# Page groups one slot ahead of the scan, first loads over three queues, last scan pair moved into the GLU

## What is computed

```
# S5: diagonal complex recurrence per group and state
x_re, x_im = cf * (B u);  first step += ab * h0
h[t] = ab * h[t-1] + x[t];  y = Re(C h) + d * u
z = gelu(y) @ w_glu + b_glu;  out = z[:, :D] * sigmoid(z[:, D:])
# compression: 8 samples x 2 pairs of KV heads, once for K, once for V
h = b1 + sum over 32 taps of rows(16 n + t) @ w1[t];  out = gelu(h) @ w2  (K: then rope)
```

## Time and profile before

| | |
|---|---|
| median of 3 runs | 3571.66 us (3571.52 to 3574.16) |
| profiled execution | 3578.02 us, its span 3576.2 us |
| TensorE, VectorE, ACT, GpSimd busy | 93%, 56%, 41%, 12% |
| mean granted TensorE clock | 0.968 |

### The profile page before, as it was taken

One profiled execution on the slowest core, in us unless ns is written; L12 is line 12 of the kernel. 1 busy time (PEld: TensorE's weight loads), 2 busy tenths in 40 slices (PEclk: granted clock), 3 DMA queues, 4 the chain that ended last, 5 costly groups with the idle time before them and its releaser, 6 DMA issues.

```text
span 3576.2 us, 71349 instructions
## 1 busy us (share of the span) xinstructions
PE 3333.5 (93%) x27932; PEld 3153.2 (88%) x27932; DVE 2019.8 (56%) x2324; ACT 1482.8 (41%) x1947; POOL 443.1 (12%) x381
## 2 busy tenths in 40 slices
PE   3999999999899999999999997888899999999998
PEld 2888888889899999999989985754689999999997
DVE  5888878765644444445664535344464444444565
ACT  2455555543444433343444431233344443334342
POOL 0555556510000000000000000000000000000000
PEclk9999999999999999999999998988899999999998
DMA  4444544445466556665455556776646655566543
GB/s 113 126 128 141 155 138 147 138 149 171 138 182 184 180 182 178 181 177 180 155 170 173 167 170 199 256 239 215 213 155 180 180 175 185 177 182 180 179 157 109
DMA packets 380155, 608.11 MB, mean 170 GB/s; under 512 B 52875, under 2 KB 138894, under 8 KB 379406
## 3 DMA queue, kind: packets, MB, share of 16 engines
q1 hardware_dynamic: 356878, 549.58, 50.5%
q10 hardware_dynamic: 23056, 55.55, 4.8%
HBM read 594.83 MB, written 26.94 MB: 174 GB/s over the span
## 4 chain that ended last, share of the span: by engine, by line
PE 74%; DVE 11%; issue 5%; POOL 4%; ACT 2%; DMA 2%; SPq 1%; ACTq 0%; POOLq 0%; DVEq 0%
PE psum L372 21%; PE psum L374 21%; PE psum L373 21%; DVE rows_rest L1134 2%; PE psum L2034 1%; DVE turned L1193 1%; PE psum L2085 1%; DMA w_raw<-in_cache_slc_k 1%; PE psum L1932 1%; PE psum L2044 1%; POOL prod_pool L1335 1%; PE psum L856 1%; DVE sumsq L448 1%; PE psum L858 1%; PE psum L857 1%
## 5 line engine op out<-in xcount | busy, mean ns | idle before, releaser
L357 DVE TENSOR_TENSOR w_rest<-w_raw,w_head 128x1024 fp32r<-128x1024 f32 x780 | 980.8, 1270 | 1061.6 <-ACT w_head L353 1056.2
L353 ACT ACTIVATE w_head<-w_raw 128x1024 fp32r<-128x1024 f32 x780 | 816.8, 1057 | 1082.5 <-PE psum L374 1029.2
L372 PE MATMUL psum<-act_head,w_head 128*128 128x264 f32 x4224 | 1209.9, 286 | 29.1 <-DVE act_rest L425 24.8
L374 PE MATMUL psum<-act_head,w_rest 128*128 128x264 f32 x4224 | 1206.6, 286 | 0.0
L373 PE MATMUL psum<-act_rest,w_head 128*128 128x264 f32 x4224 | 1205.0, 285 | 0.0
L372 PEld LDWEIGHTS psum<-act_head,w_head 128*128 128x128 f32 x4224 | 802.1, 190 | 33.3 <-issue 32.3
L373 PEld LDWEIGHTS psum<-act_rest,w_head 128*128 128x128 f32 x4224 | 804.0, 190 | 0.0
L374 PEld LDWEIGHTS psum<-act_head,w_rest 128*128 128x128 f32 x4224 | 802.3, 190 | 0.0
L372 PE MATMUL psum<-hid_head,w_head 128*128 128x264 f32 x1408 | 401.0, 285 | 0.0
L374 PE MATMUL psum<-hid_head,w_rest 128*128 128x264 f32 x1408 | 400.6, 285 | 0.0
L373 PE MATMUL psum<-hid_rest,w_head 128*128 128x264 f32 x1408 | 399.9, 284 | 0.0
(11 more groups left out here) (350 smaller groups left out, 4120.5 us busy)
## 6 DMA issues: line engine op xcount, KB each, us to landing
w_raw<-in_ffn_w_gate SPq DMA_DIRECT2D x176, 512.0 KB, 3.8
w_raw<-in_ffn_w_up SPq DMA_DIRECT2D x176, 512.0 KB, 4.3
w_raw<-in_ffn_w_down SPq DMA_DIRECT2D x176, 512.0 KB, 4.2
w_raw<-in_cache_cmp_k SPq DMA_DIRECT2D x256, 128.0 KB, 2.6
w_raw<-in_cache_cmp_v SPq DMA_DIRECT2D x256, 128.0 KB, 2.7
w_raw<-in_ssm_w_glu SPq DMA_DIRECT2D x64, 512.0 KB, 3.9
w_raw<-in_ple_w_gate SPq DMA_DIRECT2D x64, 512.0 KB, 4.3
w_raw<-in_kv_w SPq DMA_DIRECT2D x48, 512.0 KB, 4.0
```

The lines of the kernel that those rows point to most:

```text
L353: nc.scalar.activation(WH[:, u.slot, :], RAW[:, u.slot, :], ACT.Copy).then_inc(head_done, 1)
L357: nc.vector.tensor_tensor(WL[:, u.slot, :], RAW[:, u.slot, :], WH[:, u.slot, :].bitcast(F32), ALU.subtract).then_inc(rest_done, 1)
L372: nc.tensor.matmul(o, WH[:, u.slot, w], heads[:, k, :], start=k == 0, stop=False)
L374: last = nc.tensor.matmul(o, WL[:, u.slot, w], heads[:, k, :], start=False, stop=k == UK * kunits - 1)
```

## The change

- **Lead of one.** `LEAD` goes from 0 to 1: slot k now holds scan pair k-1. The loop starts at slot 0, with tap group 0 in it; page group 0 is turned in the start. Pair 31 is left over: its inputs are multiplied in slot 31, and its scan, rotation and outputs run behind the splits of the GLU's units (`glu_dve`), with `outputs_pe` at chunk 11.
- **Loads.** SP keeps identity, A, log dt, page table, iota and the state, then the pages. ACT issues x in four column quarters, the samples and the taps (into a buffer of their own, so that the page ring is free). GpSimd issues sixteen: gains, biases, masks, the second weights and rope tables.
- **The start's work.** x is copied out half by VectorE, half by ACT; squares are summed by 16 matmuls with ones in place of four VectorE reductions; tap rests go to GpSimd; the parameter chain is cut in four pieces that lie between the page rests, its last piece (`coefficients_dve`) in slot 0.
- **Order in a slot.** B and C are turned after part 2 instead of after part 1, and ACT copies them after the sines and heads 4 and 5.
- **The end.** The splits of y are spread through slot 31 and the embeddings are turned in two pairs. The final states are turned in the GLU's second step.

```diff
     def start_pe(pe):
...
+        def x_job(c):
+            if c % 4 == 0:
+                pe.wait_ge(ld_x[c // 4], 32 if c == 0 else 16)
+            if c >= 3:
+                if c - 3 < X_BY_DVE:
+                    pe.wait_ge(x_evac_dve, c - 2)
+                else:
+                    pe.wait_ge(x_evac_act, c - 2 - X_BY_DVE)
+            sl = slice(c * P, (c + 1) * P)
+            turn(x_bank(c), [(XN[:, 0, sl], 0), (XN[:, 1, sl], P), (XS[:, sl], 2 * P)]).then_inc(x_turned, 1)
+        def sums(g):
+            pe.wait_ge(sq_first, g + 1)
+            for c in range(4 * g, 4 * g + 4):
+                last = nc.tensor.matmul(PSUM[:, SUM_BANK, 0:T], ONES[:, :], SQ[:, c, :], start=c == 0, stop=c == KC - 1)
...
+        turn(7, [(AN[:, k, :], k * NQ) for k in range(3)]).then_inc(tp_done, 1)
+        for c in range(X_BY_DVE):
+            x_job(c)
+        pe.wait_ge(ld["s0"], 32)
...
+        for c in range(X_BY_DVE, KC):
+            x_job(c)
+        pe.wait_ge(ones_done, 1)
+        for g in range(4):
+            sums(g)
+            turn_pages_pe(pe, 0, 2 * g, 2 * g + 2)
+        pe.wait_ge(ld["vec"], L_VEC)
+        pe.wait_ge(x_evac_act, KC - X_BY_DVE)
+        turn(4, [(VEC[:, 0, :], 0)])
+        turn(5, [(VEC[0:50, 1, :], 0)]).then_inc(tp_done, 1)
+        pe.wait_ge(tp_evac, 3)
+        pe.wait_ge(rows_padded, 2)
     def start_dve(dve):
...
+        turns_step_dve(dve)
...
+        rests_dve(dve, 0, 0, 4)
+        turns_low_dve(dve)
+        rests_dve(dve, 0, 4, 6)
+        turns_high_dve(dve)
+        rests_dve(dve, 0, 6, 8)
+        dve.wait_ge(tp_done, 4)
...
+        rms_dve(dve, "mix0")
     def start_act(act):
+        for q in range(4):
+            sl = slice(q * 512, (q + 1) * 512)
+            act.dma_start(XN[:, :, sl], io["x_prompt"][0].rearrange("(q p) d -> p q d", p=P)[:, :, sl]).then_inc(ld_x[q], 16)
...
+        for g in range(4):
+            nc.scalar.activation(SQ[:, 4 * g:4 * g + 4, :], X[:, 4 * g:4 * g + 4, :], ACT.Square).then_inc(sq_first, 1)
+        for u in range(RING):
+            act.wait_ge(raw_ready[u], 16)
+            nc.scalar.activation(WH[:, u, :], TAPS_FIRST[:, u, :], ACT.Copy).then_inc(head_done, 1)
+            heads_act(act, 0, 2 * u, 2 * u + 2)
+        rms_act(act, "mix0")
+    def start_pool(pool):
...
+        for u in range(RING):
+            pool.wait_ge(head_done, u + 1)
+            nc.gpsimd.tensor_tensor(WL[:, u, :], TAPS_FIRST[:, u, :], WH[:, u, :].bitcast(F32), ALU.subtract).then_inc(rest_done, 1)
...
-    LEAD = 0
+    LEAD = 1
     def stage1_pe(pe):
-        rms_pe(pe, "mix0")
-        pe.wait_ge(ld["late"], L_LATE)
-        for k in range(-1, NITEM):
+        for k in range(NITEM):
             p = k - LEAD
             taps_pe(pe, k, 0)
             turn_pages_pe(pe, k + 1, 0, 2)
             taps_pe(pe, k, 1)
             turn_pages_pe(pe, k + 1, 2, 4)
-            if p >= 1 and p % 2 == 1:
-                turn_bc_pe(pe, p // 2 + 1)
+            if k == NITEM - 1:
+                turn_embeds_pe(pe, 0, DEPTH)
             taps_pe(pe, k, 2)
             turn_pages_pe(pe, k + 1, 4, 6)
             if k == NITEM - 1:
-                turn_embeds_pe(pe)
+                turn_embeds_pe(pe, DEPTH, 2 * DEPTH)
+                second_pe(pe, k - 1)
+            if p >= 1 and p % 2 == 1:
+                turn_bc_pe(pe, p // 2 + 1)
             taps_pe(pe, k, 3)
...
     def stage1_act(act):
...
             heads_act(act, k + 1, 2, 4)
-            if p >= 1 and p % 2 == 1:
-                take_bc_act(act, p // 2 + 1)
...
             heads_act(act, k + 1, 4, 6)
             if boundary:
                 split_taps_act(act, 1)
+            if p >= 1 and p % 2 == 1:
+                take_bc_act(act, p // 2 + 1)
...
     def stage1_dve(dve):
...
             rests_dve(dve, k + 1, 0, 2)
+            if k == 0:
+                coefficients_dve(dve)
             round_dve(dve, p + 1)
+            if final:
+                for c in range(6):
+                    y_rest_dve(dve, c)
+                first_units_dve(dve, 0)
             scans_dve(dve, p)
             rests_dve(dve, k + 1, 2, 4)
             if boundary:
                 split_taps_dve(dve, 0)
+            rotated_out_dve(dve, p)
             if final:
-                first_units_dve(dve, 0)
-            rotated_out_dve(dve, p)
+                rests_embeds_dve(dve, 0, DEPTH)
+                for c in range(6, 12):
+                    y_rest_dve(dve, c)
+                first_units_dve(dve, 1)
...
     def stage1_pool(pool):
         pool.wait_ge(arg_ready, N_PAR)
+        pool.wait_ge(norm_sum, 1)
+        pool.wait_ge(ld["late"], L_LATE)
...
     def glu_pe(pe):
         def first(k):
-            if k == 4:
+            if k == 0:
+                pe.wait_ge(cmp_rest, 8 * NITEM + 2 * DEPTH)
+                pe.wait_ge(cmp_out, NITEM - 1)
+                pe.wait_ge(cmp_gelu, NITEM - 1)
+            if k == 3:
                 second_pe(pe, NITEM - 1)
+            if k == 11:
+                outputs_pe(pe, NPAIR - 1)
+            if k == 12:
+                pe.wait_ge(cmp_out, NITEM)
+            pe.wait_ge(xl_done, k + 1)
...
     def glu_dve(dve):
         def split(eng, u):
+            c = u.n - ph.base - RING
             split_rest(eng, u)
-            if u.n == ph.base + RING + 4:
+            if c == 0:
+                scans_dve(eng, NPAIR - 1)
+            if c == 1:
+                rotated_out_dve(eng, NPAIR - 1)
+            if c == 2:
+                joined_out_dve(eng, NPAIR - 1)
+            if c == 3:
+                y_sum_dve(eng, KC - 1)
+            if c == 4:
+                y_rest_dve(eng, KC - 1)
+            if c == ph.per + 4:
+                dve.wait_ge(cmp_kept, 16 * NITEM)
                 states_dve(eng, 0, 4)
```

More of the change, by code:

```diff
@@ L595, in job, with x_bank, turn @@
+    SUM_BANK = 3
+    def x_bank(c):
+        return 4 + c % 3
+    def start_pe(pe):
+        def turn(bank, ins):
             for src, at in ins:
                 n, m = src.shape[0], int(np.prod(src.shape[1:]))
-                last = nc.tensor.transpose(PSUM[0:m, j % 8, at:at + n], src, IDENT[0:n, 0:n])
-            last.then_inc(tp_done, 1)
-            j += 1
-        pe.wait_ge(ld["const"], L_CONST)
-        job([(VEC[:, 0, :], 0)], (ld["vec"], L_VEC))
-        job([(VEC[0:50, 1, :], 0)])
@@ L604, in start_pe @@
-        pe.wait_ge(ld["ssm"], L_SSM)
-        job([(AN[:, k, :], k * NQ) for k in range(3)], (par_dve, 1))
-        pe.wait_ge(ld["x"], 32)
-        for c in range(KC):
-            sl = slice(c * P, (c + 1) * P)
-            job([(XN[:, 0, sl], 0), (XN[:, 1, sl], P), (XS[:, sl], 2 * P)])
-        for k in range(2):
-            job([(S0[:, k, m, :], m * P) for m in range(4)])
+                last = nc.tensor.transpose(PSUM[0:m, bank, at:at + n], src, IDENT[0:n, 0:n])
+            return last
@@ L663, in start_act @@
         act.wait_ge(par_dve, 2)
         nc.scalar.activation(PR[:, 4, :], PSF[:, 0, :], ACT.Exp).then_inc(par_act, 1)
+        for c in range(X_BY_DVE, KC):
+            act.wait_ge(x_turned, c + 1)
+            nc.scalar.activation(X[:, c, :], PSUM[:, x_bank(c), 0:T], ACT.Copy).then_inc(x_evac_act, 1)
         act.wait_ge(par_dve, 3)
@@ new lines, in trunk_kernel, with link_par, tt_par, rounded_par @@
+    X_BY_DVE = 8
+    par_steps = [0]
+    def link_par(dve, ins):
+        par_steps[0] += 1
+        ins.then_inc(arg_ready, 1)
+        dve.wait_ge(arg_ready, par_steps[0])
+    def tt_par(dve, o, a, b, op):
+        link_par(dve, nc.vector.tensor_tensor(o, a, b, op))
+    def rounded_par(dve, o, a, tmp):
+        link_par(dve, nc.vector.tensor_scalar(tmp, a, MAGIC, -MAGIC, ALU.add, ALU.add))
+        tt_par(dve, o, a, tmp, ALU.subtract)
+    def small(k):
+        return PSF[:, k, :]
+    def par(k):
+        return PR[:, k, :]
@@ L1067, in first_units_act, with y_head_act, y_rest_dve @@
         split_head(act, Unit(TAP_UNITS + u))
+    def y_head_act(act, c):
+        nc.scalar.activation(XL[:, c, :], YF[:, c, :], ACT.Copy).then_inc(xh_done, 1)
+    def y_rest_dve(dve, c):
+        dve.wait_ge(xh_done, c + 1)
+        nc.vector.tensor_tensor(XH[:, c, :], YF[:, c, :], XL[:, c, :].bitcast(F32), ALU.subtract).then_inc(xl_done, 1)
     def stage1_act(act):
-        for k in range(-1, NITEM):
+        for k in range(NITEM):
             p = k - LEAD
@@ L1406, in b, with split @@
             square_act(act, ph.sq + i, ds(4 * i, 4), x_done, i + 1)
-        after_units(act, "glu", split_head, nothing, b)
+        def split(eng, u):
+            split_head(eng, u)
+            if u.n == ph.base + RING + 4:
+                gelu_y_act(act, KC - 1)
+                act.wait_ge(y_gelu, KC)
+                y_head_act(act, KC - 1)
+        after_units(act, "glu", split, nothing, b)
     def glu_dve(dve):
```

373 lines of the change are left out of this document (181 added, 192 removed).

## The result

| | before | after |
|---|---|---|
| median of the runs | 3572.91 us (3571.52 to 3577.97, 4 runs) | 3526.78 us (3523.09 to 3532.52, 4 runs) |
| profiled execution, its span | 3578.02 us, 3576.2 us | 3525.9 us, 3524.1 us |
| TensorE busy, mean granted clock | 93%, 0.968 | 94%, 0.967 |

The kernel after takes 0.987 of the time before, with an interval of 0.9853 to 0.9887: 46 us less. I had forecast 3515. The two profiled executions differ by 52.1 us, against a sum of 57.

A forecast was written before the change was run, and what follows sets the result against it. TensorE was taken as the bound, busy 93%, so gains come only where it idles or runs slowly. 34 (start) + 22.5 (slots) + 1.2 (end) = 57.7, less added waits 57; from the median 3571.66 that gives 3515, range 3497 to 3540.

The forecast's parts named there:

- all three places: The start (gain 34 us), the slots, one per page group (22.5 us), and the end, last slot to GLU (1.2 us).
- the likeliest case: The author's own forecast: start, slots and end all gain, time 3515 us; chance 0.41.
- the slots gave 21.5: Rival in the slots: odd ones meet ACT's sines and VectorE's full queue, so slots give nothing, 3536 us; chance 0.20.
- the sums of squares sped up: Rival in the start: the sums stay slow, twelve more slow calls cost 6 us, 3521 us; chance 0.15.
- parameters and page rests didn't just trade places: Rival in the start: parameters and page rests only trade places, first inputs at 85, 3536 us; chance 0.06.
- sixteen loads: Rival in the start: GpSimd's sixteen loads delay its tap rests; slower from 5.5 us each, 3580 at 6; chance 0.04.
- The start was mis-sized: Start: first tap matmul at 46 instead of 88.18, first inputs about 71 instead of 104.85; gain 34 us, bounds 25 to 40.
- VectorE's low table (3.3): In the start, VectorE's low angle table stands between the fourth and fifth page rest and takes 3.3 us.
- The fifth page turn, due at 58.5, starts at 63.2: In slot 0, a 4.7 us stall behind coefficients (8.5 us), a table op, rounding and two rests replaces the old one.
- The slots were right: Padding wait goes; odd slots 20.6 (K half) and 20.3 (V half), waits 0.3 to 0.75; gain 22.5 us, bounds 6 to 34.
- The end: Last slot to GLU: 27.6 us instead of 28.8, third embedding waits for rests; gain 1.2 us, from -3 to 4.
- one of my signs of being wrong: Prediction wrong if the GLU's first step waits for scan 31, odd slots stay over 21.3, or first tap comes after 55.

The follow-up runs named there:

- the last group: Last set of runs timed side by side, with the kernel after repeated unchanged: 3526.35 us, ratio 0.9861, beside the kernel before at 3576.48 us.

## Why the prediction was right, and by how much not

**The mechanism** was right in all three places, and the likeliest case was the one that came. The named rivals fell: the slots gave 21.5, the sums of squares sped up (first group 3.46 us for 8 matmuls, the next 1.95), parameters and page rests didn't just trade places (first inputs at 77.45, not 85), and GpSimd issued its sixteen loads in 0.48 to 0.67 us each, done at 9.6 us. They were 20 us clear of the first tap rest. Whether a copy of VectorE can hold such a load back, as the prediction feared, was not put to the test: VectorE stood idle from 1.30 to 9.39.

**The start was mis-sized**: 27.4 us instead of 34.
- "VectorE's low table (3.3)" took 7.4, since I laid it beside GpSimd's tap rests and priced it by rows in which GpSimd stood idle. This is 4.1 us and the largest miss. GpSimd's tap rests took 2.72 each, not the 3.41 of its products, and were never waited for. The first tap at 48.79 is only 2.8 over my 46, because other steps were a little shorter, the gains and biases among them, which don't release it.
- "The fifth page turn, due at 58.5, starts at 63.2": the wait was 5.93 instead of 4.7, by the same chain, whose 8.5 us were right (56.16 to 64.66).
- The second wait in slot 0, 2.60 us, I missed; I had named one wait as the sign. I had counted GpSimd's padding for TensorE's turn of B and C, but not that the angle parts stand behind it on GpSimd, the sines behind them, and page heads behind the sines.
- x began at 10.29, not 7.5, since TensorE's queue puts A's turn first and that waited for log dt (9.81). Eight of the x turns then went at 0.52 us each instead of 0.82 and gave that back.

**The slots were right**: waits of 0.75 (K) and 0.60 (V) in odd ones, 20.74 and 20.15 against 20.6 and 20.3, no falls of the clock in slots 2 to 30 (one in slot 1, 15 matmuls from 80.42 to 83.41). K's even slots also wait 0.30, as they did before. The longest wait, 2.74 us where the V half begins, was 2.59 before; I had named neither.

**The end**: the embedding's wait was 3.77 (forecast 4.4) and the GLU waited for no y chunk. One wait of 0.64 us for pair 31 appeared in the first step, where I had ruled out any that matters. By the letter this is one of my signs of being wrong; it came at a size that decides nothing, beside 1.5 us of slow matmuls that went from the same step.

**From the sum to the time.** The profiled executions differ by 52.1, the medians by 46.1. That of before lay 5.1 over its median, that of after 0.9 under its own. I took 57 from the median; taken from the profiled execution's own 3578.02, as its durations ask for, the forecast was 3521, and half of the 12 us of error is this step. Beside each other in the last group the two kernels were 50.1 us apart (3576.48; 3526.35), as the 49.7 of the table. The start, the slots and the last slot all gave less than forecast, so these errors add up; luck is the 2.4 us of the eight faster x turns, which I hadn't foreseen and which made good x's late begin. Small slips of arithmetic (34 - 9.7 is 24.3, not 25; 23.33 - 20.6 is 2.7, not 2.8) move nothing.

## What to carry to other kernels

When two elementwise engines are given work in the same stretch, price each by a row in which the other was busy too; alone and together differed by up to five times here. A chain moved behind other work is hidden only if nothing that is due soon stands behind it in its engine's queue: moving 8.5 us of it behind the first matmuls was worth nothing, and then two instructions up 5 to 6 us. And when several edits come as one, try the smallest alone: here moving one piece of work, the turn of B and C with its copy, made 20 of the 50 us.

## What the runs showed of the hardware that I had not expected

**VectorE and GpSimd slow each other.** VectorE's step with two constants (TENSOR_SCALAR) went from 0.69 to 2.73 us, its subtraction from 1.22 to 3.25, the normed chunk from 0.48 to 2.64, while GpSimd worked on large tiles; GpSimd's subtraction went from 2.36 to 2.72. VectorE pays far more of it.

**x turns at two paces in the same code.** In nine of twelve profiles with the new start the x turns went from 0.82 to 0.52 us a job, between 18.9 and 21.1 us, after nothing but transposes; in three they stayed at 0.82 to the end, and the sums began some 2 us later. Two runs of the very same kernel, the kernel after (first) and its repeat (second):

```profile
16.86 1.97 PE L588 MATMUL psum<-ident,s_nat 128*128 128x128 f32 x8
18.62 0.53 PE L588 MATMUL psum<-ident,x_nat 128*128 128x128 f32 x2
...
19.24 0.44 PE L588 MATMUL psum<-ident,x_nat 128*128 128x128 f32 x2
...
26.22 3.46 PE L605 MATMUL psum<-squares,ones 128*128 128x264 f32 x8 [3.26 <-ACT squares L684]
```

```profile
16.84 1.97 PE L588 MATMUL psum<-ident,s_nat 128*128 128x128 f32 x8
18.60 0.64 PE L588 MATMUL psum<-ident,x_nat 128*128 128x128 f32 x2
19.37 0.69 PE L588 MATMUL psum<-ident,x_nat 128*128 128x128 f32 x2
...
28.44 2.98 PE L605 MATMUL psum<-squares,ones 128*128 128x264 f32 x6 [3.26 <-ACT squares L684]
```

From 18 to 26 us the granted clock reads 0.98 in the first and 1.00 in the second, so that row doesn't tell the two paces apart. The Trainium skill (TensorE: Matmul & The Clock Gate, "Part 4: PE-mode transpose") says that transposes don't bring the upper level; the first of these two runs speaks against it, the second alone would have agreed, as the x turns of the earlier trace rows did. Why one and not the other, no run here shows.
